# Seven block products instead of eight in the up projections of two feed-forward blocks (Trainium2, one core, fp32)

## What is computed

```python
def swiglu(h, w_in, w_out):
    gu = h @ w_in
    gate, up = gu[..., :D_FF], gu[..., D_FF:]
    return (jax.nn.silu(gate) * up) @ w_out
...
x = x + swiglu(rmsnorm(x, norm_ffn_w[i]), ffn_w_in[i], ffn_w_out[i])
```

## Time and profile before

| what | value |
|---|---|
| median of 3 runs | 1454.01 us (1453.71 to 1454.04) |
| the profiled execution | 1455.41 us |
| its span | 1453.6 us |
| granted TensorE clock, mean | 0.994 of 2.4 GHz |
| weights and other data read | 122.01 MB, 85 GB/s over the span |

### The profile page before, as it was taken

One profiled execution on the slowest core, in us unless ns is written; L12 is line 12 of the kernel. 1 busy time (PEld: TensorE's weight loads), 2 busy tenths in 40 slices (PEclk: granted clock), 3 DMA queues, 4 the chain that ended last, 5 costly groups with the idle time before them and its releaser, 6 DMA issues.

```text
span 1453.6 us, 17600 instructions
## 1 busy us (share of the span) xinstructions
PE 1429.2 (98%) x6854; PEld 1156.8 (80%) x6854; DVE 792.9 (55%) x1640; ACT 593.5 (41%) x1199; POOL 53.1 (4%) x108
## 2 busy tenths in 40 slices
PE   8999999999999999999999999999899999999998
PEld 7777766887888888888888888866688888888887
DVE  5566664566577565443454445777564443345443
ACT  5655543445454243222223333667642332223223
POOL 0111000000000000000000000011000000000000
PEclk9999999999999999999999999999999999999999
DMA  6311111132213132313323133312032222422222
GB/s 226 106 63 58 59 58 58 46 104 102 76 55 105 55 116 87 110 68 99 116 99 112 62 98 107 105 54 70 30 104 100 87 73 98 134 87 87 91 82 75
DMA packets 25922, 127.98 MB, mean 88 GB/s; under 512 B 3248, under 2 KB 5936, under 8 KB 14832
## 3 DMA queue, kind: packets, MB, share of 16 engines
q1 hardware_dynamic: 25408, 126.60, 25.7%
q10 hardware_dynamic: 432, 0.27, 0.1%
HBM read 122.01 MB, written 2.23 MB: 85 GB/s over the span
## 4 chain that ended last, share of the span: by engine, by line
PE 94%; DVE 3%; ACT 1%; DMA 1%; issue 1%; SPq 0%; POOLq 0%; DVEq 0%; POOL 0%; ACTq 0%
PE PS L608 91%; PE PS L627 1%; PE PS L869 1%; DVE FT L1648 1%; DVE WL L1211 1%; DVE FT L1211 0%; DMA FT<-rows 0%; ACT L951 0%; DVE FT L1214 0%; PE PS L845 0%; DMA RAW<-in_w_in 0%; ACT VF L951 0%; DVE FT L1217 0%; DVE FP L1217 0%; DVE G L1211 0%
## 5 line engine op out<-in xcount | busy, mean ns | idle before, releaser
L608 PE MATMUL PS<-XH,WH 128*128 128x512 f32 x1080 | 431.0, 399 | 0.9 <-ACT VF L951 0.9
L608 PE MATMUL PS<-XH,WL 128*128 128x512 f32 x1080 | 421.5, 390 | 0.0
L608 PE MATMUL PS<-XL,WH 128*128 128x512 f32 x1080 | 421.1, 390 | 0.0
L1211 DVE TENSOR_TENSOR WL<-RAW,WH 128x512 fp32r<-128x512 f32 (+1 forms) x454 | 288.5, 672 | 206.1 <-ACT WH L951 205.5
L608 PE MATMUL PS<-FR,WH 128*128 128x512 f32 (+1 forms) x1132 | 341.1, 384 | 2.0 <-DVE WL L1211 2.0
L951 ACT ACTIVATE WH<-RAW 128x512 fp32r<-128x512 f32 (+1 forms) x454 | 250.6, 607 | 177.8 <-PE PS L608 175.4
L608 PEld LDWEIGHTS PS<-FR,WH 128*128 128x128 f32 x1132 | 209.4, 189 | 44.2 <-issue 3.7
L608 PEld LDWEIGHTS PS<-XH,WH 128*128 128x128 f32 x1080 | 203.1, 188 | 47.9 <-issue 6.3
L608 PEld LDWEIGHTS PS<-XH,WL 128*128 128x128 f32 x1080 | 203.0, 188 | 43.4
L608 PEld LDWEIGHTS PS<-XL,WH 128*128 128x128 f32 x1080 | 203.3, 188 | 41.0 <-issue 1.0
L608 PE MATMUL PS<-FR,WL 128*128 128x512 f32 (+1 forms) x566 | 216.4, 382 | 0.0
(11 more groups left out here) (120 smaller groups left out, 1145.2 us busy)
## 6 DMA issues: line engine op xcount, KB each, us to landing
RAW<-in_f_in SPq DMA_DIRECT2D x44, 1024.0 KB, 4.9
RAW<-in_w_in SPq DMA_DIRECT2D x12, 1024.0 KB, 4.9
RAW<-in_m_in SPq DMA_DIRECT2D x12, 1024.0 KB, 4.9
RAW<-in_f_oa SPq DMA_DIRECT2D x16, 768.0 KB, 4.2
RAW<-in_f_ob SPq DMA_DIRECT2D x16, 640.0 KB, 3.9
RAW<-in_a_in SPq DMA_DIRECT2D x6, 1024.0 KB, 4.9
RAW<-in_w_out SPq DMA_DIRECT2D x4, 1024.0 KB, 4.8
RAW<-in_m_out SPq DMA_DIRECT2D x4, 1024.0 KB, 4.9
```

The source lines that it names most:

```text
L608: return e.matmul(o, l, r, start=start, stop=stop, skip_group_check=True)
L1211: return e.tensor_tensor(o, a, b, op)
```

## The change

Of each block's 22 chunks the first four are done as before (`PLAIN`), the other 18 by seven products. A chunk's weights (1024 by a gate tile and an up tile) are taken as 2 by 2 blocks of 512 by 128, and the normalised activations (1024 by 512 tokens) as 2 by 2 blocks of 512 by 256. Seven products of sums of such blocks give the four result blocks (Winograd's form of Strassen's scheme); each product is 4 k x 3 matmuls of 256 columns. What it takes:

- **Activations.** XN are the activations times norm weight and tokens' factor, eight DVE operations (`xn`) in the second plain chunk. After the last plain matmul ACT and DVE split three of their blocks into XH and XL in place (`bs`, six units: four of 128x256, two of 128x1024). Four sums of blocks (TT) are made on GpSimd (`ts`, 128x1024 each) and split into TH and TL (`th`), which lie over G and VF. All are made once per block, in the plain chunks.
- **Weights.** Four sums of the chunk's blocks (`ws`, 128x512 each) are made on GpSimd for each chunk, three steps ahead of its first part; one lies in RAW in place of a block. Seven parts are split instead of four, three from RAW as it is loaded, one of the sum in RAW, three of sums in FP. WH and WL become a ring of eight slots of 512.
- **Products.** Seven steps a chunk, one for each product, in PSUM banks 0 to 3 or 4 to 7 by turns, half a bank each. Products 4, 5 and 6 add onto banks 0, 2 and 3, after those have been read.
- **Sums of products.** ACT copies product 0 (`s0`); DVE adds products 1, 2, 3, 5 and 6 (`s1`, `s2`, `s3`, `s5`, `s6`), 256 wide; ACT takes the gate's Silu in two halves (`s4`, `s6`); DVE's product and ACT's copy of the hidden tile (`fmul`) and its low part (`fl`) come in the next chunk's steps. The multiplications with RB fall away.
- **Order.** Weight parts become side units, with offsets of their own; about a quarter of the other offsets change. The chunks' columns are packed in another order on the host; their size is the same.

```diff
+PLAIN = 4
+FIRST_RING = 35
...
         for j in range(2, len(self.chunks)):
             g = self.group[j]
             before = self.begin[self.group[g - 1]]
...
+            for p in range(self.parts(j)):
+                first[j] = at = max(before + p, self.free(j, p) - 1, first.get(j, 0))
+                self.side(at - 0.25, ("w", j, p))
+        for j in self.seven:
+            self.side(int(self.places["w", j, 0]) - 3, ("ws", j))
...
+                if x >= PLAIN:
+                    m = P.seven[j]
+                    b4 = 4 * (m % 2)
+                    for q in range(7):
+                        n = P.step(("seven", j, q, b4, P.bank.get(b4 + q, ()) if q < 4 else (), base), [j], q)
+                        P.ev((f"s{q}", m, l * 22 + x, b4, n))
...
+            if half == 0:
+                for i in range(8):
+                    P.side(start + 8 + i // 2, ("xn", l, i))
+                for i in range(4):
+                    P.side(start + 11 + 2 * i, ("ts", l, i))
+                    P.side(start + 14 + 4 * i, ("th", l, i))
...
+    def region(bank, q):
+        return PS[:, bank + (0, 1, 2, 3, 0, 2, 3)[q], 0:256]
...
+        def seven(j, q, bank, after, base):
+            m = P.seven[j]
+            for f in after:
+                p.wait_ge(*f)
+            p.wait_ge("wl", P.split[j, q])
+            if q in (4, 5, 6):
+                p.wait_ge({4: "p1", 5: "st", 6: "c22"}[q], m + 1)
+            l = base // 32
+            for k in range(4):
+                if q in (0, 4, 6):
+                    p.wait_ge("bsl", 6 * l + {0: k + 1, 4: 5, 6: 6}[q])
+                else:
+                    p.wait_ge("tl", 4 * l + {3: 1, 1: 2, 2: 3, 5: 4}[q])
+                o, c = region(bank, q), slice(128 * k, 128 * k + 128)
+                t = mm3(o, (WHB[:, P.slot[j, q], c], WLB[:, P.slot[j, q], c]), seven_b(q, k),
+                        q < 4 and k == 0, k == 3)
+            t.then_inc(sems["su"], 1)
...
         def w_parts(j, q):
...
+            src, high, _ = w_block(j, q)
+            if j in P.seven and q in (1, 2, 3, 6):
+                p.wait_ge("ws", 4 * P.seven[j] + {2: 1, 3: 2, 1: 3, 6: 4}[q])
+            else:
+                p.wait_ge(f"wd{j % 2}", 16 * (j // 2))
             p.wait_ge("su", P.free(j, q))
...
+        def s0(m, n, bank, su):
+            p.wait_ge("su", su)
+            p.wait_ge("fm", n - 1)
+            copy(FT[:, 6 + n % 2, 0:256], region(bank, 0)).then_inc(sems["p1"], 1)
...
+        def bs(l, i):
+            p.wait_ge("su", plain_end[l])
+            p.wait_ge("xn", 8 * l + (i + 1 if i < 4 else 8))
+            d, c = (slice(i, i + 1) if i < 4 else slice(4, 8)), slice(256, 512) if i == 5 else slice(0, 256)
+            copy(XH[:, d, c], XN[:, d, c]).then_inc(sems["bsh"], 1)
...
+        def s2(m, n, bank, su):
+            p.wait_ge("usum", m + 1)
+            p.wait_ge("su", su)
+            x = FT[:, 6 + n % 2, :]
+            tt(x[:, 0:256], x[:, 256:512], region(bank, 2), ALU.add).then_inc(sems["st"], 1)
+
+        def s3(m, n, bank, su):
+            p.wait_ge("st", m + 1)
+            p.wait_ge("su", su)
+            p.wait_ge("fhl", n - 1)
+            tt(FT[:, 2 + n % 2, 256:512], FT[:, 6 + n % 2, 0:256], region(bank, 3), ALU.add).then_inc(sems["c22"], 1)
...
+        def ws(j):
+            m = P.seven[j]
+            a = [RAW[:, j % 2, 512 * i:512 * i + 512] for i in range(4)]
+            s2, s3, s4 = (seven_w(j, q) for q in (1, 2, 6))
...
+            p.wait_ge(f"wd{j % 2}", 16 * (j // 2))
...
+            e.tensor_tensor(s3, a[0], a[2], ALU.subtract).then_inc(sems["ws"], 1)
+            p.wait_ge("ws", 4 * m + 1)
+            e.tensor_tensor(a[2], a[2], a[3], ALU.add).then_inc(sems["ws"], 1)
+            p.wait_ge("ws", 4 * m + 2)
+            p.wait_ge("wl", free[1])
+            e.tensor_tensor(s2, a[2], a[0], ALU.subtract).then_inc(sems["ws"], 1)
+            p.wait_ge("ws", 4 * m + 3)
+            p.wait_ge("wl", free[2])
+            e.tensor_tensor(s4, a[1], s2, ALU.subtract).then_inc(sems["ws"], 1)
```

More of the change, by code:

```diff
@@ L112, in __init__, with chunk, parts, part @@
         self.chunks, self.split, self.tiles, self.freed, self.bank = [], {}, [], {}, {}
+        self.slot, self.before, self.held, self.ring, self.seven = {}, {}, {}, 0, {}
         self.steps, self.begin, self.release, self.group = [], {}, {}, {}
         self.misc, self.places = {}, {}
-    def chunk(self, ap, nk, width):
+    def chunk(self, ap, nk, width, seven=False):
+        j = len(self.chunks)
         self.chunks.append((ap, nk, width))
+        if seven:
+            self.seven[j] = len(self.seven)
+        if j < FIRST_RING:
+            self.ring = 4 * (j % 2)
+        for p in range(self.parts(j)):
+            self.slot[j, p] = self.ring % 8
+            self.before[j, p] = self.held.get(self.ring % 8)
+            self.held[self.ring % 8] = j, p
+            self.ring += 1
+    def parts(self, j):
+        nk, width = self.chunks[j][1:]
+        return 7 if j in self.seven else (nk * width + 511) // 512
+    def part(self, j, k):
+        return k * self.chunks[j][2] // 512
     def wl(self, j, k):
@@ L121, in wl @@
             return 2 * next(g for g, (a, b) in enumerate(GROUPS) if a <= k < b) + j + 1
-        return self.split[j, k // 2]
+        return self.split[j, self.part(j, k)]
     def read(self, j):
-        return 9 + j if j < 2 else max(self.split[j, p] for p in range((self.chunks[j][1] + 1) // 2))
+        return 9 + j if j < 2 else max(self.split[j, p] for p in range(self.parts(j)))
     def tile(self, kind, i, j, u, bank, base):
-        t = Tile(kind, i, j, u, bank, base, self.bank.get(bank))
+        t = Tile(kind, i, j, u, bank, base, self.bank.get(bank, ()))
         self.freed[FREED[kind]] = n = self.freed.get(FREED[kind], 0) + 1
-        t.freed = self.bank[bank] = (FREED[kind], n)
+        t.freed = (FREED[kind], n)
+        self.bank[bank] = (t.freed,)
         self.tiles.append(t)
@@ L153, in free @@
     def free(self, j, p):
[L155 to L159, removed]
+        return self.release.get(self.before[j, p], 0)
     def fm(self, kind, i, j, u, bank, base):
@@ L172, in spread_weights @@
             before = self.begin[self.group[g - 1]]
-            for p in range((self.chunks[j][1] + 1) // 2):
-                at = max(before + p, self.free(j, p) - 1, first.get(j, 0))
-                self.steps[at][2].append(("w", j, p))
-                first[j] = at
-        for n, u in enumerate(u for s in self.steps for u in s[2]):
+            for p in range(self.parts(j)):
+                first[j] = at = max(before + p, self.free(j, p) - 1, first.get(j, 0))
+                self.side(at - 0.25, ("w", j, p))
+        for j in self.seven:
+            self.side(int(self.places["w", j, 0]) - 3, ("ws", j))
+        order = [u for u in sorted(self.places, key=self.places.get) if u[0] == "w"]
+        for n, u in enumerate(order):
             self.split[u[1:]] = 11 + n
@@ L183, in units @@
             sides.setdefault(int(self.places[u]), []).append(u)
-        for i, (pe, ev, w) in enumerate(self.steps):
-            out += [pe, *w, *ev, *sides.get(i, ())]
+        for i, (pe, ev) in enumerate(self.steps):
+            out += [pe, *ev, *sides.get(i, ())]
         n = 0
@@ L208, in ffn_chunks @@
             for j in range(FH):
-                P.chunk(A["f_in"][l * 22 + half * FH + j], 8, 256)
+                P.chunk(A["f_in"][l * 22 + half * FH + j], 8, 256, seven=half * FH + j >= PLAIN)
             for dp in range(4):
@@ L393, in ffn @@
     def ffn(l, j, base):
-        bank = 0
+        bank, start = 0, len(P.steps)
         for half in range(2):
@@ L410, in ffn @@
                 if x:
-                    P.side(len(P.steps) - 7, ("fl", l * 22 + x - 1))
+                    P.side(len(P.steps) - (7 if x < PLAIN else 6), ("fl", l * 22 + x - 1))
                 if l == 0 and half == 1 and f >= 2:
@@ L537, in blocks_kernel @@
     xv = A["xT"].rearrange("(k p) s -> p k s", p=128)
+    plain_end = [next(i for i, (u, _) in enumerate(P.steps) if u[0] == "seven" and u[5] == b) for b in (16, 32)]
+    seven_end = max(i for i, (u, _) in enumerate(P.steps) if u[0] == "seven") + 1
     rcol = [col(4) for _ in range(5)]
@@ L579, in hid_slot, with seven_w, seven_b, w_block @@
         return 2 * (f % FH), 2 * (f % FH) + 1
+    WHB, WLB = (W[:, :, :].rearrange("p h (q n) -> p (h q) n", n=512) for W in (WH, WL))
     def w_of(W, j, k, c):
         wdt = chunks[j][2]
-        return W[:, j % 2, k * wdt + c.start:k * wdt + c.stop]
+        at = k * wdt % 512
+        return W[:, P.slot[j, P.part(j, k)], at + c.start:at + c.stop]
+    XN = FP[:, 8:16, :]
+    TT = [FP[:, 16 + 2 * i:18 + 2 * i, :].rearrange("p a (b n) -> p (a b) n", n=256) for i in (0, 1, 2, 0)]
+    def seven_w(j, q):
+        if q in (1, 2, 6):
+            return FP[:, {1: 22, 2: 23, 6: 24}[q], :]
+        i = {0: 0, 4: 1, 3: 2, 5: 3}[q]
+        return RAW[:, j % 2, 512 * i:512 * i + 512]
```

(28 more changed lines are left out.)

162 lines of the change are left out of this document (125 added, 37 removed), and 74 rows, old and new, of the table SHIFT.

## The result

The changed kernel takes 1513.64 us (median of 4 runs, 1510.47 to 1514.13) against 1453.86 us of the kernel before (4 runs, 1450.68 to 1454.04): the ratio is 1.0412, with an interval of 1.0397 to 1.0426. It is slower by 4.1%. The profiled execution took 1514.13 us, with a span of 1512.3.

A forecast was written before the change was run, and what follows sets the result against it. TensorE's matmul stream was taken as the bound, and to stay so: 1454.0 - 29.0 (shorter stream) + 3.2 (overload) + 2.3 (transitions) = 1430.5 us. Range 1425 to 1449; chance of faster 0.81.

The forecast's parts named there:

- C: Rival, chance 0.14: exclusion makes DVE and GpSimd the bound; about 1518 us without overlap, 1456 to 1464 with overlap 1.5.
- The matmuls: Seven-product chunks: 84 matmuls at 119.9 ns, 10.07 us instead of 10.88; 29.0 us saved over 36 chunks.
- DVE's own work: Per seven-product chunk: 9 x 0.60 + 5 x 0.33 = 7.05 us back to back, covered if nothing holds DVE.
- ACT's: ACT's added work per seven-product chunk: 6.2 us of 10.07, covered.
- The GpSimd sum: Each 128x512 weight sum on GpSimd takes 1.2 us, the middle of 0.96 and 1.39; 4.8 us a chunk.
- The exclusion: DVE operations with two SBUF inputs and GpSimd operations exclude each other, mutually; DVE's sums reading PSUM run beside GpSimd.
- The overload: Seven-product chunks: 7.05 + 4.8 less 1.5 = 10.35 us on DVE, 0.28 over the chunk; 3.2 us in all, table included.
- The slack: Within runs of seven-product chunks DVE may be some 2 us late before TensorE waits.
- The transitions: After each block's fourth plain chunk TensorE idles 1.15 us for the activation split, 2.3 in all; preparation covered by half-free DVE.
- The table: Rotary table's fourteen steps on DVE in the first block's second half: 1 us added.
- Moved steps: Changed offsets of side steps: worth between -3 and +3 us, taken as 0.

The follow-up runs named there:

- e12: Changed kernel, GpSimd's sums kept, with ACT's hidden-tile copy one step later and its last Silu of a chunk behind the weight copy: 1494.31 us.
- e1: Changed kernel with GpSimd's four weight sums of each chunk 2 columns wide instead of 512: 1437.70 us.
- e3: Changed kernel with GpSimd's weight sums and its four activation sums only 2 columns wide: 1429.38 us.
- e4: Changed kernel, GpSimd's sums whole; DVE's weight low parts in seven-product chunks subtract a PSUM operand instead of the high part in SBUF: 1451.93 us.
- e9: Changed kernel with weight and activation sums on DVE, ACT's hidden-tile copy one step later, its last Silu of a chunk behind the weight copy: 1442.02 us.
- e13: e9 with the rotary table's fourteen steps moved from the first block's second-half up projections into its first down projection: 1437.01 us, ratio 0.9876.

## Why the prediction was wrong

The forecast was faster with 0.81 and the outcome is the rival with 0.14: C, that the exclusion makes DVE and GpSimd the bound. Its time with no overlap, 1518, is 4 us from what was measured, and its spacing, 12.6, close to 12.37; but it came to them by a GpSimd sum of 1.39 us and by sums from PSUM that don't run beside it, and neither is so: that nearness is luck. Its other spacing, 11.1 with an overlap, is near e12's 11.20, where the queue waits are gone. The mechanism is C's, the size has a term that no case had.

Of the 83 us between 1430.5 and 1513.64 some 64 lie in the chunks (forecast -29.0 + 3.2, measured +38.0) and some 24 in the heads (forecast 2.3, measured 26.4); the stretches outside gave 5.7 back.

Point by point:
- **The matmuls**: 119.9 ns was forecast, 118.9 measured; 9.985 us a chunk instead of 10.07. The price was right. That the stream alone sets the spacing when nothing holds it was right as well (e1, e3, e4, e9).
- **DVE's own work**, 7.05 us: right where its operations follow each other at once, 0.60 and 0.33 us between starts. With gaps between them it is 7.5 by the records of e1. **ACT's** is covered as load (22.75 of 39.94 us in e1).
- **The GpSimd sum**, 1.2 us from two bounds: 1.28 measured alone, 7% over. The 1024-wide one, taken at 2.3, takes 2.38 alone (the first of the four at 551.78) and 2.70 on average, as DVE holds up the others. By the Trainium skill ("GPSIMD Engine Reference", section "Performance versus the Vector engine") the estimate was 1.17; the trace is 9% above it.
- **The exclusion**: right, and in both directions. That DVE operations with PSUM as one input are free of it: right, shown by e4. The Trainium skill states it so ("SBUF — State Buffer", section "Who interferes with whom"), and here it stands with a number: 682 ns beside GpSimd's sums, against 1.72 us with both inputs in SBUF.
- **The overload: this step failed.** The prediction added DVE's 7.05 and GpSimd's 4.8, took off 1.5 and held "Counted from DVE: ... 10.35" against the period of 10.07. Measured: 12.16 over four chunks, 12.37 in the long run. Two things are wrong with it, of about equal weight. First, it took all of DVE's idle time as usable, and put at nothing the waits at the head of in-order queues, DVE for ACT's weight copies, ACT for DVE's product: 2.2 us which recur every chunk, 7.05 + 2.9 + 2.2 = 12.15. Taking them away by order alone gives 1.0 us a chunk back (12.16 to 11.20, e12). Second, the sum without them is too low: 11.20 in e12 where it says 10.35, since DVE's own work takes up to 7.5 and it is held for 3.4 us. The 2.9 us of the change are below the 3.3 that were allowed only because one GpSimd sum in four ran inside a wait. So with hardly a queue wait left the forecast would still have been wrong in direction (e12: 1494.31 us).
- **What the trace before could have told.** In the feed-forward stage, from 550 to 640 us, DVE waited like this:

```profile
DVE WL L1211 <- ACT WH L951: 9.7, 8, 1.2
```

That is one wait of 1.2 us a chunk. Added to the prediction's sum it makes 11.55, over the plain chunk's 10.88, and the sign of the forecast turns. It is half of what the change then had (2.2), so the size would still have been missed, and such a wait costs nothing where the engine has time to spare (e1). Over the whole kernel the same wait is the 200.2 us of the earlier trace rows, which were read for the durations only.
- **The slack** "DVE may be some 2 us late": in the second block's first run the starts of the second products are 10.9 and 11.7 us apart (1171.09, 1181.96, 1193.62), from the third chunk on it is 12.37. Some 2 us of slack, then, right in size, but gone after two chunks of an overload of 2.4 a chunk instead of 0.28.
- **The transitions**, 2.3 us in all: measured some 26. The working had preparation covered by "DVE has half free", the same error as above; GpSimd's 11 us of 1024-wide sums held DVE in the plain chunks. That is about half of it: with no new work on GpSimd (e9) the two heads still take 6.2 and 6.7 us over 44.9.
- **The table**, 1 us: 5.0 (e13 against e9).
- **Moved steps**, "I take 0", between -3 and +3: the stretches outside the two blocks took 5.7 us less in e3, 3.8 ahead of the first and 1.8 between them. The size was off, in the change's favour; no run shows which of the moved steps did it.
- **e3 against the forecast.** Without GpSimd's sums it takes 1429.38 us, the forecast was 1430.5. That nearness is luck in part: by its stretches 32.2 us come off in the chunks, 5.7 outside, and 11.9 are lost, 8.6 of them waits at the two heads (7.4 for XL, 1.2 for TL), most of the rest low clock behind them.

Not settled: what the 6 us at each head of e9 and e13 consist of, and why each matmul costs 12 to 13 ns beyond its columns (at 2.4 GHz) at both widths.

## What to carry to other kernels

Loads that fit a period are not enough. Where two in-order engines wait for each other, look up how long the engine that gets new work waits in the stage in question, and hold load plus wait against the period. If the sum is over, try another order first; the wait costs nothing only while the engine has time to spare. A sum given to GpSimd beside a DVE that reads SBUF twice holds DVE for about 1.0 us of its 1.28 (1.72 and 1.73 us instead of 0.69): the four of a chunk cost DVE 2.9 us here and 3.4 in e12, and 2.2 when it made them itself. Two causes can cover each other, so the effect of each has to be measured with the other present and with it gone: an experiment that takes the contention away (one input from PSUM) and one that only reorders do that.

## What the hardware showed beyond that

TensorE's clock fell at the heads. The end of the first block's head, behind the waits of 0.83 and 3.39 us and with the one of 5.67 in it (the clock is the last figure but two):

```profile
570.00:584.40 14.40, 8.62 (x33) 6.23 (x31) 11.86 (x17) 9.18 (x17) 4.74 (x4) 0.86 0.21 73
```

and the 15.5 us behind it:

```profile
584.50:600.00 15.50, 14.96 (x106) 14.49 (x106) 14.64 (x18) 6.53 (x11) 5.46 (x4) 0.85 0.20 69
```

The granted clock is 0.85 there and 1.00 in the steady chunks. By their starts, the 256-column matmuls just behind the wait are 0.21 us apart (0.119 elsewhere), the 1.2 GHz level. An estimate from these rows: a clock of 0.85 over 15.5 us is 4.65 us at half speed, and half of it lost, some 2.3 us that the stall costs on top of its 5.7. This stall at the head of a stage is dearer than its wait says.
